# Projections of a hybrid decoder step: the order of the six matmuls that share a weight block

## The reference, cut to what matters

```
for layer in range(2):
    x += 0.5 * swiglu_1(rms(x))            # gate, up: 1024x2816 each; down: 2816x1024
    x += mixer(rms(x))                     # layer 0: mLSTM, layer 1: gated DeltaNet
    x += cross_attend(rms(x), mem_k, mem_v)  # w_q, w_o: 1024x1024; w_k, w_v on 256 memory tokens
    x += 0.5 * swiglu_2(rms(x))
y = rms(x)

def swiglu(h, w_gate, w_up, w_down):
    return (silu(h @ w_gate) * (h @ w_up)) @ w_down
```

## Time and profile before

| | |
|---|---|
| median of 3 runs | 2870.57 us (2869.45 to 2872.04) |
| the profiled execution's own time | 2872.99 us |
| its span, first to last instruction | 2871.0 us |
| PE busy with matmuls | 2738.6 us, 95% of the span |
| PEld (weight loads, beside the matmuls) | 2625.3 us, 91% |
| DVE busy | 1302.4 us, 45% |
| ACT busy | 893.4 us, 31% |
| mean granted clock of TensorE | 0.965 of full |
| matmuls of the projections with 260 columns | 17664 = 6 x 2944 |
| matmuls of the `memkv` phases with 256 columns | 768 |

### The profile page before, as it was taken

How to read it: one execution, slowest core, us unless ns; L and a number is a source line. 1 busy time by engine, 2 the same in 40 slices (tenths; PEclk the granted TensorE clock), 3 DMA queues, 4 the chain that set the end, 5 groups by cost and what they waited for, 6 DMA issues and landing times.

```text
span 2871.0 us, 49901 instructions
## 1 busy us (share of the span) xinstructions
PE 2738.6 (95%) x21498; PEld 2625.3 (91%) x21498; DVE 1302.4 (45%) x2082; ACT 893.4 (31%) x1125; POOL 193.6 (7%) x169
## 2 busy tenths in 40 slices
PE   7999999998979999999999999998998889999999
PEld 7999999877876999999999999998987876999998
DVE  5444234234574444432444424777334573444422
ACT  4332222233323333322222222543323232333322
POOL 2000000011110100000000000001311000100000
PEclk9999999997999999999999999999978989999999
DMA  4333334122483233332333332223213472333331
GB/s 120 93 90 104 93 90 104 45 60 67 132 275 121 73 89 93 92 101 80 88 91 92 103 89 70 74 63 88 45 52 103 145 238 96 89 90 93 99 100 51
DMA packets 472628, 278.58 MB, mean 97 GB/s; under 512 B 24821, under 2 KB 460790, under 8 KB 472459
## 3 DMA queue, kind: packets, MB, share of 16 engines
q1 hardware_dynamic: 449720, 230.83, 28.4%
q0 software_dynamic: 8704, 33.56, 3.3%
q10 hardware_dynamic: 14078, 12.35, 1.4%
HBM read 259.21 MB, written 17.69 MB: 96 GB/s over the span
## 4 chain that ended last, share of the span: by engine, by line
PE 86%; DVE 5%; ACT 3%; issue 3%; DMA 1%; POOL 0%; ACTq 0%; SPq 0%; DVEq 0%; POOLq 0%
PE ACC L429 24%; PE ACC L431 24%; PE ACC L430 24%; PE ACC L1115 2%; PE M L2119 1%; ACT w_hi L512 1%; PE ACC L2119 1%; DVE w_lo L518 1%; PE M L1449 1%; PE M L1474 1%; DVE cache L1211 1%; PE M L2258 1%; PE M L2196 1%; DMA raw<-in_xa_w_k 1%; PE M L1519 1%
## 5 line engine op out<-in xcount | busy, mean ns | idle before, releaser
L429 PE MATMUL ACC<-xg_hi,w_hi 128*128 128x260 f32 x3968 | 1132.6, 285 | 11.6 <-DVE w_lo L890 7.6
L431 PE MATMUL ACC<-xg_hi,w_lo 128*128 128x260 f32 x3968 | 1126.6, 284 | 0.0
L430 PE MATMUL ACC<-xg_lo,w_hi 128*128 128x260 f32 x3968 | 1123.2, 283 | 0.0
L518 DVE TENSOR_TENSOR w_lo<-raw,w_hi 128x1024 fp32r<-128x1024 f32 (+1 forms) x326 | 421.9, 1294 | 1060.4 <-ACT w_hi L512 1054.5
L429 PEld LDWEIGHTS ACC<-xg_hi,w_hi 128*128 128x128 f32 x3968 | 753.3, 190 | 13.4 <-issue 8.6
L430 PEld LDWEIGHTS ACC<-xg_lo,w_hi 128*128 128x128 f32 x3968 | 752.6, 190 | 0.0
L431 PEld LDWEIGHTS ACC<-xg_hi,w_lo 128*128 128x128 f32 x3968 | 752.3, 190 | 0.0
L512 ACT ACTIVATE w_hi<-raw 128x1024 fp32r<-128x1024 f32 (+1 forms) x326 | 363.6, 1115 | 1234.4 <-PE ACC L431 1223.6
L430 PE MATMUL ACC<-hid_lo,w_hi 128*128 128x260 f32 x1408 | 398.3, 283 | 0.0
L431 PE MATMUL ACC<-hid_hi,w_lo 128*128 128x260 f32 x1408 | 397.6, 282 | 0.0
L429 PE MATMUL ACC<-hid_hi,w_hi 128*128 128x260 f32 x1408 | 397.4, 282 | 0.0
(11 more groups left out here) (549 smaller groups left out, 3307.7 us busy)
## 6 DMA issues: line engine op xcount, KB each, us to landing
raw<-in_ffn_w_gate SPq DMA_DIRECT2D x88, 512.0 KB, 3.8
raw<-in_ffn_w_up SPq DMA_DIRECT2D x88, 512.0 KB, 3.8
raw<-in_ffn_w_down SPq DMA_DIRECT2D x64, 704.0 KB, 4.5
cache<-in_cache_mem_k POOLq DMA_DIRECT2D x16, 1024.0 KB, 7.2
cache<-in_cache_mem_v POOLq DMA_DIRECT2D x16, 1024.0 KB, 6.7
raw<-in_gd_w_in SPq DMA_DIRECT2D x32, 512.0 KB, 4.1
raw<-in_ml_w_in SPq DMA_DIRECT2D x24, 512.0 KB, 3.9
raw<-in_xa_w_q SPq DMA_DIRECT2D x16, 512.0 KB, 4.5
```

The source lines that it names most:

```text
L429: pe.matmul(out, wh, hi[:, k0 + k, m], start=begin, stop=False)
L430: pe.matmul(out, wh, lo[:, k0 + k, m], start=False, stop=False)
L431: mm = pe.matmul(out, wl, hi[:, k0 + k, m], start=False, stop=end)
L518: dve.tensor_tensor(w_lo[:, j % 2, 0:n], raw[:, (j + d) % 4, 0:n], w_hi[:, j % 2, 0:n].bitcast(F32), ALU.subtract).then_inc(w_split, 1)
```

## The change

In `pe_unit` the loop over the two halves, which held all three matmuls, becomes three loops over the halves, one for each matmul. For a weight block the order before was (high weight, half 0), (high weight, half 0), (low weight, half 0), then the same for half 1. Now it is high weight for half 0 and half 1, high weight (low activations) for half 0 and half 1, low weight for half 0 and half 1. The same 17664 matmuls are issued, each on the same data, bank and flags, and each bank sees its matmuls in the order of before. The `memkv` phases have one half and keep their order. Line numbers behind `pe_unit` move by two; L430 and L431 become L431 and L433.

```diff
                 if extra:
                     extra(k)
-                for h in range(1 if ph.kind == "memkv" else 2):
-                    if ph.kind == "memkv":
-                        out, m = ACC[:, 2 * pair, 0:NMEM], slice(0, NMEM)
-                    else:
-                        out, m = ACC[:, 2 * pair + h, 0:TH], slice(h * TH, h * TH + TH)
+                if ph.kind == "memkv":
+                    sides = [(ACC[:, 2 * pair, 0:NMEM], slice(0, NMEM))]
+                else:
+                    sides = [(ACC[:, 2 * pair + h, 0:TH], slice(h * TH, h * TH + TH)) for h in range(2)]
+                for out, m in sides:
                     pe.matmul(out, wh, hi[:, k0 + k, m], start=begin, stop=False)
+                for out, m in sides:
                     pe.matmul(out, wh, lo[:, k0 + k, m], start=False, stop=False)
+                for out, m in sides:
                     mm = pe.matmul(out, wl, hi[:, k0 + k, m], start=False, stop=end)
             mm.then_inc(mm_done, 1)
```

## The result

The changed kernel takes 2880.32 us (median of 7 runs, 2878.60 to 2887.01); the kernel before, in 7 runs beside it, 2871.30 us (2869.20 to 2872.04). The ratio is 1.0035, with a 95% interval from 1.0024 to 1.0046: the change costs 7 to 13 us. The forecast was 2871 us within 2862 to 2883 us. The time lies inside the range, but the case I held likeliest, no change within 0.2%, did not come: the whole interval lies above it.

What follows compares the result with a forecast made beforehand. PE bounds the kernel, through what each projection matmul costs or PE's waits. The profiled 2872.99 us plus 0 for the new order, less 2.4 us to the median, gave 2870.6, rounded to 2871 us; range 2862 to 2883 us.

Steps and rivals of the forecast that it cites:

- the case I held likeliest: Whole kernel: time stays within 0.2% of before, 2864.8 to 2876.3 us; chance 73%.
- What bounds the kernel, and the price of a matmul: PE, busy 95% of the span; projection matmuls take about 119.6 ns at full clock, 11.3 ns of it not streaming columns.
- the slower case: Rival, 13%: each of 11776 added bank changes in the projections costs 0.66 to 7.8 ns, +11.6 to +92 us.
- Equal weights are worth 0.03 ns, a bank change nothing: Steps between projection matmuls: 119.94 and 119.95 ns for the compared pair, 115.24 and 115.27 ns in memkv, so 0 us.
- the pair that before didn't have: Step between matmuls with equal weights but another bank: 0 per block before, 4 after.
- the middle step's 0.65 ns: Step L430 to L431 is 0.65 ns shorter, put down to which tile is streamed or loaded; counted as 0.
- The bounds: Equal-weight and bank-change prices over 2944 blocks: -8.1 us from steps on hid, +11.6 us from steps over all operands.
- The faster one: Rival, 11%: equal weights pay only when the bank changes too, saving up to 133 us (2738 us), or partly, 2862 us.
- The clock one: Rival, 3%: alternation makes PE pause and its clock fall, 97 ns per caught matmul; a tenth of them +171 us.

Runs made afterwards that it cites:

- e3: Changed kernel's order of banks and streamed tiles, but half 1 takes the weight block of k+1, so no neighbours have equal weights; ratio 1.0037 to before, block 720.4 ns.
- e1: Kernel before with its order of weights and streamed tiles, but the bank alternates at every matmul; ratio 0.9997 to before, block 718.3 ns.
- e5: Kernel before, order kept, with xg_hi and xg_lo interleaved in one tensor, rows of k 4160 bytes apart instead of 2080; ratio 0.9997 to before.
- e6: Changed kernel with half 1 streaming from column 256 instead of 260, 16 bytes earlier; ratio 1.0109 to before, block 728.5 ns.
- e10: Changed kernel with 32 unused bytes after xg_lo, moving weights and the region behind but not xg; ratio 1.0021 to before, block 720.6 ns.
- e11: Changed kernel with gate and up weight blocks 544 bytes apart instead of 512, so the row-to-weight distance is 224 for all k; ratio 0.9997 to before.
- e2: Changed kernel's order of weights and tiles, but matmuls 1 to 3 write one bank and 4 to 6 the other; ratio 1.0036 to before, block 720.4 ns.
- e12: e4's order with gate and up weight blocks 544 bytes apart, distance 64 bytes for all k; 2867.44 us against 2869.16 for before, ratio 0.9989.
- e4: Against before, a snake order of the six matmuls with four equal-weight neighbours and two bank changes; ratio 1.0011, block 717.3 ns.
- e7: Kernel before's order with the 520 tokens split into 256 and 264 columns instead of 260 and 260; ratio 1.0030 to before, block 718.7 ns.
- e8: Changed kernel's order with the 520 tokens split into 256 and 264 columns; ratio 1.0004 to before, block 720.7 ns.
- e9: Kernel before's order of weights and banks, but all six matmuls of a block stream the same half, chosen by weight slot; ratio 1.0029 to before.
- run 256: Not a run label: the words say that the memory phases run matmuls of 256 columns, in 115.3 ns each.

## Why the prediction was right or wrong

**What bounds the kernel, and the price of a matmul**: right. PE's waits stayed, and the loss stands in the windows at clock 1.00 as a lower count, the sign that I had named for the slower case (835 in 100 us, or 1667 in 200, instead of 837 to 839, or 1675; I had put the mark at 830, too far off for an effect of 0.3%).

**Equal weights are worth 0.03 ns, a bank change nothing**: right, and now shown for the pair that before didn't have. e3 against the changed kernel: 0.0 ns for four equal neighbours. e1 against before: 0.0 ns for four bank changes.

**"The new order streams and loads each tile as often as the old", so the middle step's 0.65 ns cancels**: this is the step that failed. I had seen that steps on xg and on hid deviate in opposite directions and concluded that the deviation belongs to tiles, and that tiles are only permuted. It belongs to which rows and weight blocks follow each other, with a pattern that goes by their distance modulo 256 (e5, e6, e10, e11). A permutation changes that sequence. The price, which the forecast set to 0, measured 2.1 ns per block: 6.1 us from the steps.

**The bounds**: the mean of the steps by kind had hidden the pattern. Split by k, before's own trace shows block sums from 714 to 723 ns (the table above), a spread of 9 ns in a kernel whose matmuls are all alike. That was there to be seen. A difference of up to 9 ns per block that no theory of mine explained should have lowered the 73% for "same". The upper bound of +11.6 us was reasoned from bank and weights, which have no part in it; that the result lies under it owes something to luck.

**The rivals**: the slower one came by sign and by size of its low end, but not by its mechanism, which e1 and e2 refute. The faster one (equal weights pay once the bank changes too) is refuted by e3. The clock one, as I put it, did not come: granted clock 1.00 in the windows, and 200 of the 17664 projection matmuls start at the lower level, against 210 before. The mean clock of the whole did fall, outside the projections (below).

**The Trainium skill**: its page "TensorE: Matmul & The Clock Gate", section "Step-by-step: what each phase is for", says that TensorE reads the streamed operand and the weights through two independent ports, so that loading the next weights takes no read bandwidth from the running matmul. The runs differ: a shift of the weights against xg by 32 bytes moves the dear block (e10), and a constant distance removes it (e11). By two fully independent reads the distance between them should be worth nothing; here the block sums range from 710 to 740 ns with it. The measurement decides.

**What stays open.** Why just these distances are dear, and how a block depends on its neighbours, isn't settled; that two reads of SBUF get into each other's way is the natural reading, but no run shows it directly.

Of the 7 to 13 us, the steps give 6. For the rest the record points to the mean granted clock, which sums up how long the kernel runs at the lower level (columns: span, clock), for before, the changed kernel and e12:

```profile
core 0: 2871.0 us, clock 0.965
...
core 0: 2878.9 us, clock 0.962
...
core 0: 2873.8 us, clock 0.960
```

In these traces before spends 201 us at the lower level and the changed kernel 219 us, the difference in the phases around the projections. How much time goes with the clock can be read from the kernel before alone: over its 88 runs beside the experiments, with clocks from 0.960 to 0.968, a clock lower by 0.001 goes with 2.5 us more, and with that taken out the runs of one group scatter by 1.1 to 1.3 us instead of 4.4 to 5.4 (standard deviations). The experiments can be compared at equal clock by this slope, an estimate (us against before; block difference times 2944, difference of the mean times, the same at equal clock with a 95% interval):

| kernel | by its steps | mean time | at equal clock |
|---|---|---|---|
| e1 | -0.1 | -0.5 | -0.3 (+-1.1) |
| e2 | +6.2 | +8.0 | +4.0 (+-1.4) |
| e3 | +6.2 | +8.6 | +3.5 (+-1.4) |
| e4 | -3.0 | +3.3 | -3.3 (+-1.0) |
| e5 | +0.5 | +0.8 | +1.0 (+-1.0) |
| e6 | +29.8 | +32.7 | +27.8 (+-1.4) |
| e7 | +1.0 | +6.0 | +0.7 (+-1.1) |
| e8 | +6.9 | +3.9 | +4.4 (+-0.9) |
| e9 | +2.2 | +10.2 | +1.3 (+-1.6) |
| e10 | +6.8 | +5.9 | +5.2 (+-1.2) |
| e11 | -0.1 | -1.6 | -0.7 (+-0.8) |
| e12 | -6.6 | -2.7 | -6.2 (+-0.9) |

With the clock taken out, whole times and steps agree within 3 us for all twelve, where the mean times as they stand miss by up to 8 us. e2, e3 and e10, which have the new order, lose 4 to 5 us at equal clock; for the changed kernel itself this can't be worked out, since the seven runs of before beside it have no clock on record. Why a kernel gets the lower clock for longer isn't shown. It doesn't follow the order alone: e8 and e10 have the changed kernel's order and the clock of before (0.964 and 0.964, against 0.964 and 0.965 of the runs beside them), while e7 and e9 have the weight order of before and a lower one (0.962 and 0.961).

## What to carry to other kernels

When a kernel is a dense stream of matmuls, compare orders by the number of matmuls in a window at full clock with no idle time: such counts repeat within 2 in 1670 here, while the whole times of one kernel spread over 0.6 to 0.8% with the granted clock. Compare whole times only together with that clock. Before you call a permutation free, split the step times by every index that changes an address; a regular pattern over that index is a price that the permutation can redistribute. Changing the PSUM bank at each matmul, or putting equal weights behind each other, bought and cost nothing here.

## What the runs showed of the hardware that I had not expected

- The spacing of 260-column matmuls at full clock depends on the distance between the streamed row and the weight block modulo 256 bytes, and on the blocks before: block sums from 710 to 740 ns for the same six matmuls (changed kernel), all at 716.3 to 716.6 ns once the distance is constant (e11).
- At constant addresses blocks can still alternate between 712 and 717 ns, and the turn of the two differs from phase to phase (e12).
- Moving one half's start by 16 bytes, all else equal, costs 1.1% per matmul here (720.4 to 728.5 ns per block) and 24 us of steps (e6).
- Four more bank changes per six matmuls: 0.0 ns (e1, and e2 in reverse). Four equal neighbours against none: 0.0 ns (e3).
- Splitting 520 columns into 256 and 264 gives 117.8 and 121.8 ns, the same pair as 260 and 260 (e7), although the memory phases run 256 columns in 115.3 ns.
- Of the spread of the whole times of one kernel, nearly all goes with the mean granted clock: 2.5 us per 0.001 (88 runs of before).
